# A two-layer hybrid decoder trunk: the first Strassen pairs and the seam into the down projection, with products, taps and quarter loads placed in another order

## The reference, cut to what matters

```python
def _conv_ffn(x, w_up, conv_w, conv_b, w_down):
    u = x @ w_up                                   # 1040 x 1024 @ 1024 x 5632
    u = sum(conv_w[2 - j] * _shift(u, j) for j in range(3)) + conv_b
    gate, val = jnp.split(u, 2, axis=-1)           # 2816 columns each
    return (jax.nn.silu(gate) * val) @ w_down      # 2816 x 1024
# in each layer, before and after it:
h = _layer_norm(ALPHA * h + mixed @ w_out, ln1_g, ln1_b)
h = _layer_norm(ALPHA * h + _conv_ffn(h, ...), ln2_g, ln2_b)
```

## Time and profile before

| | us |
|---|---|
| Median of 3 runs | 3827.04 |
| Lowest and highest of them | 3826.34, 3832.24 |
| The profiled execution's own time | 3830.86 |
| Its span from first to last instruction | 3829.1 |
| Mean granted TensorE clock in it | 0.987 |
| PE busy in the span | 3636.7 (95%) |
| Fast pairs of layer 0, of layer 1 | 1247 to 1666, 3129 to 3549 |
| Down projection of layer 0, of layer 1 | 1667 to about 1880, 3550 to 3782 |

### The profile page before, as it was taken

How to read it: one execution, slowest core, us unless ns; L and a number is a source line. 1 busy time by engine, 2 the same in 40 slices (tenths; PEclk the granted TensorE clock), 3 DMA queues, 4 the chain that set the end, 5 groups by cost and what they waited for, 6 DMA issues and landing times. The chain is left out here.

```text
span 3829.1 us, 71300 instructions
## 1 busy us (share of the span) xinstructions
PE 3636.7 (95%) x29883; PEld 3293.8 (86%) x29883; DVE 2331.4 (61%) x3009; ACT 1338.0 (35%) x1993; POOL 1174.5 (31%) x640
## 2 busy tenths in 40 slices
PE   7998999999999899999999999999999989999898
PEld 6566998988898899999985679898869979999897
DVE  2255456655569777767523544485655697777665
ACT  5255124312213344443332531351231144444434
POOL 4042420000252555534401424100004525555341
PEclk9999999999999999999999999999999999999999
DMA  4465236522322222263325732454224122222632
GB/s 115 126 188 150 70 125 192 156 69 79 123 81 79 67 84 73 84 251 122 89 58 144 220 91 95 144 176 137 68 81 139 50 78 79 83 78 86 251 122 75
DMA packets 472718, 438.10 MB, mean 114 GB/s; under 512 B 104859, under 2 KB 396919, under 8 KB 472423
## 3 DMA queue, kind: packets, MB, share of 16 engines
q1 hardware_dynamic: 452168, 382.09, 33.4%
q10 hardware_dynamic: 20255, 51.78, 3.6%
HBM read 296.76 MB, written 137.05 MB: 113 GB/s over the span
## 5 line engine op out<-in xcount | busy, mean ns | idle before, releaser
L259 POOL TENSOR_TENSOR w_hi<-w_raw,consts 128x1024 fp32r<-128x1024 f32 (+1 forms) x78 | 125.0, 1603 | 1415.0 <-DMA w_raw<-in_w_proj_rwkv 850.0
L213 PE MATMUL psum<-h_hi,w_hi 128*128 128x348 f32 x1632 | 353.8, 325 | 6.7 <-SPq L1189 4.6
L213 PE MATMUL psum<-h_lo,w_hi 128*128 128x348 f32 x1632 | 348.8, 322 | 0.0
L213 PE MATMUL psum<-h_hi,w_lo 128*128 128x348 f32 x1632 | 348.0, 322 | 0.0
L213 PEld LDWEIGHTS psum<-h_hi,w_hi 128*128 128x128 f32 x1632 | 275.9, 189 | 12.9 <-SPq L1189 5.0
L213 PEld LDWEIGHTS psum<-h_lo,w_hi 128*128 128x128 f32 x1632 | 277.2, 189 | 0.0
L213 PEld LDWEIGHTS psum<-h_hi,w_lo 128*128 128x128 f32 x1632 | 275.2, 188 | 0.0
L2665 PE MATMUL psum<-t_hi,piece_hi_w 128*128 128x260 f32 x1280 | 259.5, 284 | 14.0 <-issue 14.0
L2665 PE MATMUL psum<-t_lo,piece_hi_w 128*128 128x260 f32 x1280 | 259.4, 284 | 0.0
L2665 PE MATMUL psum<-t_hi,piece_lo_w 128*128 128x260 f32 x1280 | 258.3, 283 | 0.0
L2624 POOL TENSOR_TENSOR piece_lo_w<-sum,piece_hi_w 128x512 fp32r<-128x512 f32 x120 | 210.1, 1750 | 140.2 <-ACT piece_hi_w L2933 137.1
(11 more groups left out here) (533 smaller groups left out, 9047.9 us busy)
## 6 DMA issues: line engine op xcount, KB each, us to landing
w_raw<-in_w_in SPq DMA_DIRECT2D x68, 512.0 KB
wsum<-in_w_down SPq DMA_DIRECT2D x88, 256.0 KB
wsum_scratch<-wsum SPq DMA_DIRECT2D x22, 1024.0 KB
raw_g<-in_w_up SPq DMA_DIRECT2D x40, 512.0 KB, 3.8
raw_v<-in_w_up SPq DMA_DIRECT2D x40, 512.0 KB, 3.8
gate_scratch<-gst ACTq DMA_DIRECT2D x32, 522.0 KB, 2.9
gbuf<-gate_scratch SPq DMA_DIRECT2D x32, 522.0 KB, 3.5
prep_scratch<-prep ACTq DMA_DIRECT2D x8, 2080.0 KB
```

The source lines that it names most:

```text
L213: last = nc.tensor.matmul(bank[:, n, :], w(k), x(k)[:, nrange(n)], start=(k == 0 and q == 0), stop=(k == kt - 1 and q == 2))
L259: nc.gpsimd.tensor_tensor(w_hi[s][:, 0:width], w_raw[s][:, 0:width], consts[:, 4:5].broadcast_to([P, width]), ALU.mult).then_inc(hi_done.s ...
```

## The change

The first part of it concerns the first pairs. ACT takes the value product of pair 1 out of PSUM before `gated(1)`, not after it, and makes four of pair 2's high parts (S3, S4, t4, A22) after R1 of pair 2. `gated(2)` comes after R1 of pair 3. DVE does the gate taps of pair 1 ahead of all weight sums of pair 2, puts sums 3 and 4 behind `token_low(2)`, and does the value taps of pair 1 right after U2 of pair 2.

The second part concerns the seam. In the last pair P5 is computed before P2. ACT makes the high parts of tiles 6 to 10 before the last value tap. SP loads the first five tiles of `zq` and the first six of `xq` right after the `acc` loads, before the last store of `f`; the rest of `zq`, `xq` and `yq` follow in halves, each after the weights of a unit. The order of the steps P2 and P5 in the semaphore's count goes with it.

The third part joins semaphores to free two for the halves: the loads of the group norm's weights and its bonus now count on one (`g_all_in`), so PE waits for all three of them, and the two flags at DVE's residual sum on another.

```diff
-        pe_n = [... for p in FAST for n in PRODUCTS]
+        LAST_ORDER = ("P1", "P6", "P5", "P2", "P7", "P3", "P4")
+        pe_n = [... for p in FAST for n in (PRODUCTS if p < LAST else LAST_ORDER)]
# SP, the group norm's loads
-                sp.dma_start(wg0 ...).then_inc(w_g_in, 16)      # wg1 the same
-                sp.dma_start(bon_in ...).then_inc(bonus_in, 16)
+                sp.dma_start(wg0 ...).then_inc(g_all_in, 16)    # wg1, bon_in the same
...
-                pe.wait_ge(w_g_in, 32)
+                pe.wait_ge(g_all_in, 48)
# SP, the seam
                 for k in BACK_LAST:
                     acc_back(k)
+                sp.wait_ge(f_out[1], 16 * (FT // 2 - 1))
+                (za, zb), (xa, xb) = CUTS[0], HALVES[0]
+                sp.dma_start(zq[:, za:zb, :], quarter(za, zb, 1, 1)).then_inc(z_q_in[0], 16)
+                sp.dma_start(xq[:, xa:xb, :], quarter(xa, xb, 0, 0)).then_inc(x_q_in, 16)
                 f_store(LAST)
                 for u in range(3, NU):
                     down_unit(u)
                     if u == 3:
-                        for b in range(2):
-                            sp.wait_ge(f_out[b], 16 * (FT // 2))
-                        for n, (lo, hi) in enumerate(CUTS):
-                            sp.dma_start(zq[:, lo:hi, :], quarter(lo, hi, 1, 1)).then_inc(z_q_in[n], 16)
+                        sp.wait_ge(f_out[1], 16 * (FT // 2))
+                        za, zb = CUTS[1]
+                        sp.dma_start(zq[:, za:zb, :], quarter(za, zb, 1, 1)).then_inc(z_q_in[1], 16)
                     if u == 4:
-                        sp.dma_start(xq[:, :, :], quarter(0, KF, 0, 0)).then_inc(x_q_in, 16)
-                    if u == 5:
-                        sp.dma_start(yq[:, :, :], quarter(0, KF, 0, 1)).then_inc(y_q_in, 16)
+                        xa, xb = HALVES[1]
+                        sp.dma_start(xq[:, xa:xb, :], quarter(xa, xb, 0, 0)).then_inc(x_rest_in, 16)
+                    if u in (5, 6):
+                        ya, yb = HALVES[u - 5]
+                        sp.dma_start(yq[:, ya:yb, :], quarter(ya, yb, 0, 1)).then_inc((y_q_in, y_rest_in)[u - 5], 16)
# PE
-                    block_product(p, A12, 0, ...)
+                    if p < LAST:
+                        block_product(p, A12, 0, ...)
                     block_product(p, S1, 4, ...)
+                    if p == LAST:
+                        block_product(p, A12, 0, ...)
# ACT
                 weight_high(NCONV, A12)
                 weight_high(NCONV, S1)
-                weight_high(NCONV, S3)
-                weight_high(NCONV, S4)
-                t_high(4)
-                weight_high(NCONV, A22)
+                taken(1, "v")
                 gated(1)
-                taken(1, "v")
                 for p in FAST:
                     first_out(p)
+                    if p == NCONV:
+                        weight_high(p, S3)
+                        weight_high(p, S4)
+                        t_high(4)
+                        weight_high(p, A22)
+                    if p == NCONV + 1:
+                        gated(NCONV)
                     gate_out_(p)
...
                         weight_high(p + 1, A22)
-                        gated(p)
+                        if p > NCONV:
+                            gated(p)
...
                 fast_tap(LAST, "g")
+                for k in range(6, KF):
+                    piece_high(0, k)
                 fast_tap(LAST, "v")
                 slot_high(2)
-                for k in range(6, KF):
-                    piece_high(0, k)
# DVE
                 product_of(0)
+                conv(1, "g")
                 dve.wait_ge(pes.sem, pes.of(0, "g0"))
                 nc.vector.memset(row(NCONV, "ug")[:, 0:2], 0.0).then_inc(pads, 1)
-                for n in range(1, 5):
-                    weight_sum(NCONV, n)
+                weight_sum(NCONV, 1)
+                weight_sum(NCONV, 2)
                 token_low(2)
-                conv(1, "g")
+                weight_sum(NCONV, 3)
+                weight_sum(NCONV, 4)
                 token_low(1)
                 token_low(3)
                 for p in FAST:
                     block_sum(p, "U2")
+                    if p == NCONV:
+                        conv(1, "v")
                     block_sum(p, "R5")
...
                     if p == NCONV:
-                        conv(1, "v")
                         product_of(1)
```

## The result

| | before | changed |
|---|---|---|
| Median, us (five runs each) | 3831.02 | 3812.66 |
| Lowest and highest | 3826.34, 3832.24 | 3809.06, 3813.83 |
| Span of the profiled execution | 3829.1 | 3808.2 |

The ratio is 0.9949, 95% interval 0.9938 to 0.9960. That is 19.5 us of 3831, where 30.2 were forecast; the two medians differ by 18.4. 3812.66 lies inside 3786 to 3814, 1.3 us from its end. Of its distance to 3796.8, 4 us are the kernel before itself, whose median over five runs is 3831.02, not 3827.04.

The account below looks back on a forecast made before the run. PE's waits in the first pairs (behind ACT and DVE) and at the seam bound the gain: 19.2 + 11.0 = 30.2 us off 3830.86 gives 3800.7, or 3796.8 for the median from 3827.04; range 3786 to 3814.

Parts of the forecast that it names:

- P6: Pair 2, PE's wait for cv1: starts at 3133.05; 1.5 us of the 7.47 stay and 6.0 go.
- R1 of pair 3: First pairs: R1 ends at 3160.9, so P2 of pair 3 starts 9.5 us earlier, including P6's 6.0.
- Half clock behind P2 of pair 3: After a gap of about 4 us the clock may fall; charged at 0.8 us.
- A: Stage from pair 2's P1 to the end of the last P4; forecast gain 8.8 and 10.4 us (layers 0, 1).
- unit 3's restart at the seam: Seam: weights land at 3573.3, PE restarts at 3578.0 instead of 3578.63, after waiting 4.5 us.
- Half clock at the seam: Seam: the 4.5 us gap before unit 3 may bring half clock, priced at 0.6 us.
- S: Stage from the end of the last P4 to unit 6's first matmul; forecast gain 5.5 us a layer.
- (b): Rival, first pairs: DVE slowed by POOL, 11 us gap before P2 of pair 3; 3813 us; chance 0.12.
- (e): Rival, first pairs: P6 waited for something other than cv1, R1 alone gives 2 to 3 us; 3810; chance 0.05.
- (a): Rival, seam gives nothing: unit 3 at 3581.5 or later, units 4 and 5 wait as before; 3807.8; chance 0.17.
- (c): Rival: both clock losses vanish, unit 3 comes at ACT's floor; 43 us gained, 3784; chance 0.09.
- (d): Rival, seam: quarters ahead of the last store run at 235 GB/s, unit 3 restarts at 3589; 3837; chance 0.05.

Follow-up runs that it names:

- e11: Changed kernel, POOL's low parts of pairs 2 and 3 cut to 64 of 512 columns: P2 of pair 3 starts 25.89 us after P1.
- e12: Changed kernel with unit 2's high part on ACT right after the last gate tap: unit 3 restarts 31.1 and 31.2 us after the last P4.
- e7: Changed kernel plus nine identity matmuls on PE before unit 3's weights: unit 3 takes 8.0 us; ratio 0.9933.
- e4: Changed kernel with first halves of zq and xq asked for after unit 3's weights: ratio 0.9950.
- e5: Changed kernel with unit 3's weights right after zq's first half, xq's first half after the last store of f: ratio 0.9935.
- e9: Changed kernel with unit 3's weights before the last store of f and unit 4's right after, then the quarters: ratio 0.9913.
- e6: Changed kernel with unit 2's high part behind the last SiLU on ACT: unit 3 restarts 31.2 us after the last P4 in both layers.

## Why the prediction was right, and where its sizes were off
The way and the waits were right; of both stages the gain was forecast too large, 10.1 us in all. The time lies inside the range by a small margin, and not because the sum was close.

**P6: right.** The wait is for `cv1`, 1.5 us were to stay, 1.30 stayed in layer 1 and none in layer 0. The swap alone showed it.

**R1 of pair 3: right in kind, the size near.** P2 of pair 3 was to start 32.4 us after P1 in layer 1 (3161.0 less 3128.55); it starts at 34.0, and at 31.7 in layer 0. With POOL shortened it starts at 25.9, where PE's own work sets it, so POOL cost P2's start 8.1 and 5.8. DVE's own list lost more. I had counted 27.4 us for it without POOL and charged 8 for POOL; it took 37.2 from pair 0's product to C21 in layer 1 and 38.1 in layer 0, a loss of 9.8 and 10.7. In layer 0 the list began 3.2 us earlier against P1, so less of it reached P2. The count of 27.4 itself holds: in `e11` the same stretch, less its waits for PE, takes 27.9.

**A wait that I had at 0.7 us came at 1.69 and 2.46** (layer 0, layer 1): P3 for R5. I had spread POOL's slowdown evenly; in fact three quarters of it, 7.3 of 9.8 us, fell ahead of U2, 4.2 of them on `token_low(1)` and `token_low(3)`, eight in 9.40 for 5.22. Since PE then reaches P2 of pair 3 later, the gap there is 3.57 and 2.21, not 4; the two share one cause, and R5 moved ahead only moved the wait. It cost nothing at P2, and neither did the half clock behind it.

**Half clock behind P2 of pair 3** was charged at 0.8 us. Against the 377.0 us that the rest of A takes without it, it cost 2.4 in layer 0 and 1.5 in layer 1. A fell short of the forecast gain by 1.4 in layer 0, all of it this; in layer 1 by 2.2, of which 1.5 is the later P2 and 0.7 this.

**The term that was mis-sized is unit 3's restart at the seam**, 28.7 us after the last P4 in my sum, 31.32 and 31.03 measured. It has two parts.
- The last store of `f` was put at 16 us and went out at 17.5, since one of DVE's taps took 4.32 beside POOL's `slot_d` instruction. I had named this collision, at the product, and taken the middle. It cost nothing: with the store at 15.8 the weights landed 0.2 us later (`e12`).
- The queue was put dry of quarters at 19.9 us after the last P4, the store and the weights moved by 23.0, and the weights landed at 24.0. They landed at 26.35. The first half of `xq` landed 19.3 us after its issue at 3533.74, that is at 22.9; the queue's rate fell from 347 to 65 GB/s between 3553.5 and 3555.0, at about 24.3. So some 1.3 us are the queue's and 1.0 is the step from there to the landing, for which I had added 1 us without a row and which took 2. Of the queue's part, 0.7 can be the old kernel's: I had let it be full to 3563, while its rate fell between 3563.0 and 3564.5, and ACT saw the last `acc` load at 3565.4. The rest stays open; that `ring_a`'s earlier start saved the 1 us that I took off for it isn't shown.

**Half clock at the seam** was priced at 0.6 us, from no row, and cost 2.0 to 2.2 (`e7`). The length of the wait, 6.6 us and not 4.5, doesn't explain it: behind waits of 2.0 to 3.5 us in `e4` and `e5` unit 3 took 9.7 us for 7.9. Restart and clock make 2.3 + 1.6 us in layer 1, where S fell short by 3.8. In layer 0 it fell short by 2.7, since the stage before was 1.1 longer there than in layer 1, for which the sum was made.

**The rest of the seam: right.** The waits for `ring_a` and `ring_c` fell to 0.5 and nothing, units 4 to 6 had none, unit 5 and 6 followed at 7.9 us. The joined semaphores cost nothing that shows.

**The rivals.** (b), 3813, lies nearest to 3812.7, then (e), 3810, and (a), 3807.8, all nearer than the forecast's 3796.8; so the time alone would have chosen the wrong mechanism. (b) wanted a gap of 11 us before P2 of pair 3 and its start 40.5 us after P1, and it came at 31.7 and 34.0 after gaps of 3.57 and 2.21. (Its own working, 27.4 and 19 us from 3122.98, gives 3169.4 for C21, not 3168.) (e) is refuted by the swap. (a), the seam gives nothing, has its reason in unit 3 only: waits of 4.2 and 4.9 us at units 4 to 6 are gone, and from unit 3's restart to unit 6's 3.0 and 3.4 us were gained, half clock included. (c)'s ends, no clock loss and unit 3 at ACT's floor, did not come; `e5` has the floor at 26.5 and 26.8 us, not 25.4. (d)'s rate is refuted: the quarters ahead of the store ran at 397 GB/s from 3546 to 3552, not 235, and the restart came 2.3 and 2.6 us later than in my sum, not 11. The Trainium skill's rule of ring order (DMA: Bandwidth & Descriptors, "Queues, rings and completion order") holds in `e12`, where an earlier issue landed no earlier. The Trainium skill's rule of the lock (SBUF — State Buffer, "SBUF: two separate sides") holds for single instructions, a tap of 4.32 us beside one of 3.24. For a long list the 19 us that I took from it overstate: 9.8 and 10.7 measured.

## What to carry to other kernels
Where a restart names no releaser, look in the other engines' lists for what ended 0.1 us before it: here two lines in the wrong order held PE for 6.0 of 7.5 us, and one swap gave over half of the part. A transfer that is asked for early is paid for by all that stands behind it in the same queue (2.9 MB made 8.5 us of 5.6); put the weights of the next product first, then what the later ones need, and price it by the time at which the queue runs dry. After a list is packed tight, look for the engine that slows it: DVE's eight subtractions took 5.2 us with POOL's instructions cut short and 9.4 beside the whole ones. And where the rivals' times lie within a few us of each other, as here, only a named restart tells them apart.

## What the runs showed of the hardware
- A tap on DVE (`scalar_tensor_tensor`, 1.31 us) took 4.32 us when a POOL subtraction of 3.24 us ran across it, and the product behind it 4.09 when the order changed: one instruction of POOL can cost DVE 3 us at a place where it matters, though a list of 27.4 us took 37.2 beside POOL, 1.4 times. Why a list loses less than its single instructions do wasn't tried.
- PE's gaps of 1.9 to 2.5 us had both outcomes. A gap of 2.46 us was followed by half clock in layer 1 of the changed kernel and not in layer 0 of `e6`; one of 1.97 before unit 3 was in `e5`, one of 1.99 in `e9` was not. What decides between them stays open.
- The part of the span that no edit touches varied by 11.6 us over fourteen traces; a 5 us effect needs the stage's own length, not the span of one execution.
